# A hybrid decoder step: attention values two units behind their scores, the gate's projection partly between the dilated units, and the sample's values in three buffers

## What is computed

```python
u = rmsnorm(x) @ w_in                       # 1024 -> 4992 columns, 13 slabs of 384
# gated recurrence (hgrn), 6 heads: output o_a, gate g = silu(u[:, gate slab])
# differential attention, 6 heads, two maps, 512 keys, causal
a = softmax(q1 k1) - lam * softmax(q2 k2);  o_b = a @ v
# dilated sliding windows, 4 heads, dilations 1, 4, 16, merged by their denominators
o_c = sum_g w_g * (softmax(q_g k_g) @ v_g)
mix = concat(rmsnorm(o_a) * g, rmsnorm(o_b) * c, o_c)
h = x + mix @ w_out
h = h + experts(rmsnorm(h))                 # 16 experts, 2 of them for each token
y = final_norm(h + sigmoid(rmsnorm(h) @ pgw) * (p @ ppw))
```

## Time and profile before

| what | us |
|---|---|
| median of 3 runs (lowest, highest) | 1104.04 (1103.67, 1109.15) |
| time of the profiled execution | 1108.18 |
| its span | 1106.4 |
| TensorE busy / weight loads | 1039.1 (94%) / 542.3 |
| VectorE, ScalarE, GpSimd busy | 367.7, 249.1, 91.1 |
| DMA | 214.92 MB, mean 194 GB/s |

### The profile page before, as it was taken

The page is one execution under the profiler, slowest core; times in us unless marked ns, Lnnn a source line. Parts: engine busy times, 40 slices in busy tenths (PEclk is TensorE's granted clock), DMA queues, the critical chain, the costliest instruction groups (busy, mean ns, idle before and its releaser), DMA issues.

```text
span 1106.4 us, 11357 instructions
## 1 busy us (share of the span) xinstructions
PE 1039.1 (94%) x4147; PEld 542.3 (49%) x4147; DVE 367.7 (33%) x766; ACT 249.1 (23%) x577; POOL 91.1 (8%) x113
## 2 busy tenths in 40 slices
PE   6998999999998999888899969999999999998896
PEld 3444455544454765564644544444444444444342
DVE  5017436533225557255631341111011110100453
ACT  3043222211222322442421110001000100011454
POOL 1000000000005342010010010000000000001200
PEclk9998999988999999989999969999999999999999
DMA  6735303304346462346353285689998999886401
GB/s 200 285 133 162 131 3 133 133 3 164 133 139 230 153 212 61 113 154 198 122 199 123 77 318 194 241 305 343 350 345 305 343 348 341 286 330 250 134 20 57
DMA packets 97099, 214.92 MB, mean 194 GB/s; under 512 B 14481, under 2 KB 42996, under 8 KB 96668
## 3 DMA queue, kind: packets, MB, share of 16 engines
q1 hardware_dynamic: 86288, 185.78, 47.9%
q0 software_dynamic: 5616, 19.89, 5.0%
q10 hardware_dynamic: 5148, 8.63, 2.1%
HBM read 191.97 MB, written 41.14 MB: 211 GB/s over the span
## 4 chain that ended last, share of the span: by engine, by line
PE 81%; DVE 7%; DMA 3%; ACT 3%; SPq 2%; issue 2%; POOL 1%; ACTq 0%; DVEq 0%; POOLq 0%
PE ps L1967 15%; PE ps L2393 10%; PE ps L2423 10%; PE ps L2399 10%; PE ps L1972 7%; PE ps L2292 5%; PE ps L2488 5%; PE ps L2262 2%; PE ps L2003 2%; PE ps L1975 2%; PE ps L2049 1%; PE ps L2076 1%; PE ps L2188 1%; PE ps L1978 1%; SPq L636 1%
## 5 line engine op out<-in xcount | busy, mean ns | idle before, releaser
L1967 PE MATMUL ps<-xT,EXPERT 128*128 128x512 f32 x384 | 184.1, 623 | 1.5 <-DVE EXPERT L1298 1.5
L1972 PE MATMUL ps<-EXPERT,xT 128*128 128x384 f32 (+1 forms) x384 | 119.6, 454 | 0.0
L2393 PE MATMUL ps<-EXPERT,aF 128*128 128x512 f32 x256 | 114.7, 601 | 1.3 <-DVE aF L1856 1.3
L2423 PE MATMUL ps<-EXPERT,dF 128*128 128x512 f32 x256 | 112.6, 593 | 1.6 <-ACT dF L1171 1.6
L2399 PE MATMUL ps<-EXPERT,aF 128*128 128x512 f32 x256 | 112.5, 592 | 0.0
L1967 PEld LDWEIGHTS ps<-xT,EXPERT 128*128 128x128 f32 x384 | 71.3, 197 | 82.2 <-issue 79.0
L1972 PEld LDWEIGHTS ps<-EXPERT,xT 128*128 128x128 f32 x384 | 78.1, 237 | 25.6 <-issue 3.6
L2393 PEld LDWEIGHTS ps<-EXPERT,aF 128*128 128x128 f32 x256 | 49.4, 193 | 63.8 <-issue 62.1
L2423 PEld LDWEIGHTS ps<-EXPERT,dF 128*128 128x128 f32 x256 | 48.6, 190 | 62.6 <-issue 60.7
L2399 PEld LDWEIGHTS ps<-EXPERT,aF 128*128 128x128 f32 x256 | 47.4, 190 | 53.6 <-issue 53.6
L2488 PE MATMUL ps<-EXPERT 128*128 128x512 f32 x128 | 56.0, 594 | 2.7 <-DVE EXPERT L1913 2.7
(11 more groups left out here) (431 smaller groups left out, 1174.3 us busy)
## 6 DMA issues: line engine op xcount, KB each, us to landing
EXPERT<-in_moe_w_gate SPq DMA_DIRECT2D x16, 2048.0 KB, 15.1
EXPERT<-in_moe_w_up SPq DMA_DIRECT2D x16, 2048.0 KB, 20.0
EXPERT<-in_moe_w_down SPq DMA_DIRECT2D x16, 2048.0 KB, 10.0
EXPERT<-in_w_in SPq DMA_DIRECT2D x13, 1536.0 KB, 6.8
out_win_sample<-in_cache_win SPq DMA_DIRECT2D x16, 1022.0 KB
Yd<-wk ACTq DMA_DIRECT2D x16, 512.0 KB, 8.4
aF<-in_cache_k_diff SPq DMA_DIRECT2D x32, 192.0 KB, 2.5
aF<-in_cache_v_diff SPq DMA_DIRECT2D x32, 192.0 KB, 2.5
```

Of the source, the lines that this page charges most:

```text
L1967: last = t.matmul(ps[:, u % 2, :], W_[:, c, c0:c0 + w], xT[:, c, 0:SEQ], start=(c == 0), stop=(c == DC - 1))
L1972: last = t.matmul(ps[:, u % 2, 0:w], rows_, W_[:, c, c0:c0 + w], start=(c == 0), stop=(c == DC - 1))
L2393: last = t.matmul(ps[:, 2 + 2 * b, :], xgT[b][:, c, :], wg_[b][:, c, :], start=(c == 0), stop=(c == DC - 1))
L2423: last = t.matmul(ps[:, 6 + hf, :], hT[b][:, c, :], wd_[b][:, c, hf * 512:(hf + 1) * 512], start=(c == 0), stop=(c == FC - 1))
```

## The change

It sets the transposes two units behind the scores and the value products three, in both attention stages, with three probability buffers; takes the maximum of unit n before `weigh(n-1)`; splits `dec_new` in `dec_pre` and a short `dec_new`; moves `dec_soft` to the end of the differential stage (in banks 2 and 3 instead of 0 and 1, so that dilated unit 0 uses banks 4 and 5, and unit 1 waits for the sample's maxima); leaves the last fifteen parts of the gate's slab (ten of tokens, four of samples and the sum) for the first dilated units, two after each step; gives the sample's values a third buffer; gives key rows four stages; loads `w_out` as three chunks, two later (`w_more`) and three (`w_rest`); moves `gate_fn` behind `dec_v(1)`, `gate_mul` behind `dec_v(3)` and the readouts behind `dec_v` 5, 8, 11 and 14; and keeps the residue statistics in a small tile, so that each store of `res_d` is two transfers. The dilated units come out like this: projection up to unit 4; `krows` and `dec_wt` in units 4 and 5; `dec_v(0)` in unit 6; `gate_fn` in unit 7; readouts in units 10, 12, 14 and 15.

```diff
-D_SHARE = 1.7
+D_SHARE = 1.55
+C_SHARE = 2
-Q_LAG, Q_EVERY = 11, 5
+Q_LAG, Q_EVERY = 16, 4
-BUSY = 4
-RO_EVERY = 10
+BUSY = 3
...
-        if 1 <= n <= nd:
-            d.append(("d_t", n - 1))
-        if n >= 2:
-            d.append(("d_pv", n - 2))
+        if 2 <= n < nd + 2:
+            d.append(("d_t", n - 2))
+        if n >= 3:
+            d.append(("d_pv", n - 3))
...
+    side = [("krows", u) for u in range(KR_EARLY)] + [("dec_wt",)] + [("dec_v", u) for u in range(2 * NS)]
+    beside = {("dec_v", 1): ("gate_fn",), ("dec_v", 3): ("gate_mul",)}
+    beside.update({("dec_v", 5 + 3 * i): ("ro", i) for i in range(NT)})
...
+        if fresh == 2 and todo[0][0] > summed[10] + 1:
+            fresh = 1
+            steps.append(("dec_pre",))
+        if fresh == 1 and todo[0][0] > summed[12]:
+            fresh = 0
             steps.append(("dec_new",))
...
+        if st == ("d_pv", nd - 2):
+            steps.append(("dec_soft",))
...
+    def beside_units():
+        kind = side.pop(0)
+        steps.append(kind)
+        if kind[0] == "dec_v" and kind[1] % 2:
+            b = kind[1] // 2
+            if b + 3 < NS:
+                steps.append(("cached", b + 3, 1))
+            if b + 4 == NS:
+                steps.append(("w_rest",))
+            if b == 3 * (NS // 3) - 1:
+                steps.append(("w_more",))
+        if kind in beside:
+            steps.append(beside.pop(kind))
+        return kind[0]
+
+    free = 0
     for k, st in enumerate(c):
         steps.append(st)
+        if k == 1:
+            steps.append(("dec_norm",))
         if todo:
+            for _ in range(min(C_SHARE, len(todo))):
+                project_one()
+            if not todo:
+                steps += [("cached", 2, 1), ("outputs",)]
+                free = k + 1
+        elif side and k >= free:
+            free = k + C_PACE.get(beside_units(), 1)
...
             def cached(b, kv):
-                buf, ld = b % 2, kvload[b % 2]
+                buf = b % 3 if kv else b % 2
+                ld = vload[buf]
                 if kv == 0 and b >= 2:
                     sp.wait_ge(S_["kused"], b - 1)
                 elif kv == 1 and b < 2:
                     sp.wait_ge(S_["kused"], NS - 1 + b)
+                elif kv == 1 and b == 2:
+                    sp.wait_ge(S_["unit_pe"], NU)
                 elif kv == 1:
-                    sp.wait_ge(S_["pv_pe"], 2 * (b - 1))
+                    sp.wait_ge(S_["pv_pe"], 2 * (b - 2))
...
-                    pool.dma_start(res_d.rearrange("(s r) n -> r s n", r=4)[x], resid[:, x]).then_inc(S_["res_st"], 16)
+                    to = res_d.rearrange("(s r) n -> r s n", r=4)[x]
+                    pool.dma_start(to[:, 0:256], resid[:, x]).then_inc(S_["res_st"], 16)
+                    pool.dma_start(to[:, 256:CW], rst[:, x]).then_inc(S_["res_st"], 16)
...
             def d_s(n):
-                if n:
-                    weigh(n - 1)
                 K = (n // HB + 1) * P
...
                                 AX.X, ALU.max, negate=True).then_inc(S_["d_max"], 1)
+                if n:
+                    weigh(n - 1)
...
-                elif n >= 2:
+                elif n == 1:
+                    pe.wait_ge(S_["row_ok"], 1)
+                else:
                     pe.wait_ge(S_["c_exp"], n - 1)
...
-                for _ in range(BUSY):
+                for _ in range(BUSY if n >= 4 else 0):
                     t.matmul(ps[:, 6, 0:2 * P], identb[:], mband[:], start=True, stop=True)
...
             def krows(u):
                 i, groups = KU[u]
                 if u == 0:
-                    pe.wait_ge(S_["row_ok"], 1)
+                    pe.wait_ge(S_["unit_ok"], NU)
...
             def dec_soft():
                 pe.wait_ge(S_["kused"], NS)
                 pe.wait_ge(S_["dec_row"], 1)
-                pe.wait_ge(S_["unit_ok"], NU)
+                pe.wait_ge(S_["d_exp"], NT * HB - 1)
```

More of the change, by code:

```diff
@@ new lines, in schedule @@
+        if fresh == 1 and todo[0][0] > summed[12]:
+            fresh = 0
+            steps.append(("dec_new",))
+        if st == ("d_t", nd - 2):
+            steps += [("dec_q", b) for _, b in keys] + [("cached", b + 2 - NS, 1) for _, b in keys]
+            keys = []
+        if st == ("d_pv", nd - 2):
+            steps.append(("dec_soft",))
+    assert not fresh and todo
+    def beside_units():
[12 more added lines that the diff above has]
+        return kind[0]
@@ L252, in schedule @@
[L252 to L257, removed]
-    for kind in side:
-        steps.append(kind)
-        if kind[0] == "dec_v" and kind[1] % 2 and kind[1] // 2 + 2 < NS:
-            steps.append(("cached", kind[1] // 2 + 2, 1))
+            for _ in range(min(C_SHARE, len(todo))):
+                project_one()
@@ L262, in schedule @@
+            if not todo:
[3 more added lines that the diff above has]
+            free = k + C_PACE.get(beside_units(), 1)
+    while side:
+        beside_units()
     steps.append(("dec_out",))
-    steps += [("ro", i) for i in range(n_ro, NT)]
     late = [("krows", u) for u in range(KR_EARLY, n_kr)]
@@ L371, in hybrid_kernel @@
         stK = work2.rearrange("p (b c v) -> p b c v", b=NS, c=3)
-        part = [kdil[0].rearrange("p g n -> p (g n)")[:, 0:SLAB], work[:, 2 * SEQ:2 * SEQ + SLAB]]
+        part = [kdil[0].rearrange("p g n -> p (g n)")[:, 0:SLAB], spart[:]]
+        wrow = wk[:].rearrange("p a n -> p (a n)")
+        dP = [wrow[:, k * 2 * SEQ:(k + 1) * 2 * SEQ] for k in range(3)]
+        cP = [wk[:, 0, 0:SEQ], wk[:, 1, 0:SEQ], wk[:, 0, SEQ:2 * SEQ]]
         kpage = [aF_[:, k * PAGES * SLAB:(k + 1) * PAGES * SLAB].rearrange("p (j n) -> p j n", j=PAGES)
                  for k in range(2)]
+        kv3 = EXPERT[:, DC * SLAB:DC * SLAB + PAGES * SLAB]
+        kd3 = EXPERT[:, DC * SLAB + PAGES * SLAB:DC * SLAB + PAGES * SLAB + 512]
+        vpage = kpage + [kv3.rearrange("p (j n) -> p j n", j=PAGES)]
+        vdil = [[k[:, g] for g in range(NG)] for k in kdil] + [[kd3[:, 0:256], kd3[:, 256:512], spart[:, 0:256]]]
+        LAST3 = max(b for b in range(NS) if b % 3 == 2)
         NQ = SLAB + NG * 256
@@ L562, in hybrid_kernel @@
         KPER = 2 * PAGES // 2 + NG
+        V3_LOADS = 16 * KPER * len([b for b in range(NS) if b % 3 == 2])
         Q_STORES = 16 * 10
@@ L662, in outputs, with w_rest, w_more @@
                             out(rows_, cvT[:, g, i])
-            does = dict(slab=load_slab, copy=copy, state_in=state_in, state_out=state_out, q_out=q_out, cached=cached,
+            def w_rest():
+                wo = a["w_out"][0].rearrange("(c p) n -> p c n", p=P)
+                sp.wait_ge(S_["c_s_pe"], NCU // 2)
+                sp.wait_ge(S_["kr_pe"], KR_EARLY)
+                for c in range(WO_NOW, DC):
+                    sp.dma_start(wout_[c], wo[:, c]).then_inc(S_["woload_last"], 16)
+            def w_more():
+                sp.wait_ge(S_["pv_pe"], 2 * (LAST3 + 1))
+                wo = a["w_out"][0].rearrange("(c p) n -> p c n", p=P)
+                sp.dma_start(EXPERT[:, WO_FIRST * D:WO_NOW * D].rearrange("p (c n) -> p c n", c=WO_NOW - WO_FIRST),
+                             wo[:, WO_FIRST:WO_NOW]).then_inc(S_["woload"], 16)
+            does = dict(w_more=w_more, w_rest=w_rest, slab=load_slab, copy=copy, state_in=state_in, state_out=state_out, q_out=q_out, cached=cached,
                         outputs=outputs)
@@ L1684, in _ @@
             does = dict(act_fn=act_fn, log_f=log_f, gate_fn=gate_fn, lev_d=lev_d, lev_q=lev_q, lev_cp=lev_cp, io_a=io_a, io_b=io_b, h_state=h_state,
-                        d_s=d_s, d_t=d_t, c_s=c_s, c_pv=c_pv, dec_new=dec_new, dec_q=dec_q, dec_soft=dec_soft, dec_norm=dec_norm, gate_mul=gate_mul,
+                        d_s=d_s, d_t=d_t, c_s=c_s, c_pv=c_pv, dec_pre=dec_pre, dec_new=dec_new, dec_q=dec_q, dec_soft=dec_soft, dec_norm=dec_norm, gate_mul=gate_mul,
                         dec_wt=dec_wt, dec_v=dec_v, dst_v=dst_v, dst_new=dst_new, dst_o=dst_o, dec_sum=dec_sum, ro=ro)
```

166 lines of the change are left out of this document (75 added, 91 removed).

## The result

The changed kernel took 1111.25 us (median of 20 runs), the kernel before, on the same chip, 1105.79 (20 runs): ratio 1.005, 95% interval 1.0032 to 1.0068. It is slower by half a per cent, where I had forecast 1% faster: +5.5 us in place of -10.2. The profiled execution took 1110.56 us, its span is 1108.8.

A forecast was written before the change was run, and what follows sets the result against it. TensorE was taken as the bound, with 32 of 289 us in waits and low clock. Terms 171.2 + 22.2 + 27.5 + 42.7 + 5.5 + 9.8 = 278.9 against 289.1, -10.2 us, gave 1093.8 us; range 1080 to 1104.

The forecast's parts named there:

- the pace of the key buffers: Differential stage: an 18.3 us round for two samples just fits 2 times 9; priced at nothing, at most 1.5 us each.
- Rival C: Differential stage: `dec_q` becomes the pace, loads meet others, six samples 1.5 us late each, 9 us; 1103 us, chance 0.16.
- the moved gate parts: Differential stage: 17.4 us of gate slab leave it, not saved but done between dilated units 0 to 4; stage 171.2 us.
- units 0 to 3: First dilated units: 5.6 us of their own and 16.6 of projection, 22.2 us, with no wait.
- the third unit of distance: Differential stage: a late VectorE can catch up; 5.7 us of waits and 1.9 of clock go, 1.0 left for remnants.
- Units 4 to 9: Dilated stage: 24.1 us of work plus waits, together 27.9, taken as 27.5 us.
- The value buffers: Dilated stage: three buffers for the sample's values remove the 5.0 us of waits for values.
- The last stretch: Unit 10's scores to last value product: 30.3 us of work, 12.4 of waits, 5.5 of clock; VectorE's load 39.2.
- my sign: Last stretch: TensorE waits for merges 10 us or more in all, at units 10, 12, 14; VectorE over 0.85 busy.
- A: Last stretch: VectorE's pile does not hold TensorE back, 38.1 in place of 48.2 us; 1083.7 us, chance 0.24.
- The low clock: Last stretch: for 12 us of waits, the worst earlier rate, 0.13 x 42.7 = 5.5 us.
- Rival B: Last stretch: clock falls with the first wait and stays at 1.2 GHz, +18 us; 1111.6 us, chance 0.10.

The follow-up runs named there:

- e14: Changed kernel with GpSimd's two large products of each sample replaced by five plain fills of the same length: 1104.82 us, 0.999 of the kernel before.
- e8: Changed kernel, `dec_q` at 11 and 5, differential transposes one unit behind scores, value products two, weighing before maximum: 1108.53 us, 0.998 of the kernel before.
- e4: Changed kernel with `dec_q` at the old 11 and 5, and gate function, its scaling and readouts moved: 1092.64 us, 0.985 of the kernel before.
- e2: Kernel before with only the new cadence of `dec_q`, first after 16 steps, then every 4: 1114.19 us, 1.005 of the kernel before.
- e6: Changed kernel with `dec_q` first 11 steps after `q_out`, but still every 4 steps: 1110.01 us, 1.000 of the kernel before.
- e16: Changed kernel with `dec_q` at 11 and 5, but `dec_q(4)` alone three steps earlier: 1102.39 us, 0.992 of the kernel before.
- e1: Changed kernel with only `dec_q` back at the old cadence, first after 11 steps, then every 5: 1097.98 us, 0.990 of the kernel before.
- e17: Changed kernel in which GpSimd first frees VectorE, then multiplies as much on an unread tile, a repeat run: 1103.42 us, 0.995 of the kernel before.

## Why the prediction was wrong, step by step

**The step that failed** is the pace of the key buffers: "18.3 us for two samples, against 2 times 9. So the pace just holds, and I price it at nothing, with up to 1.5 us for each of six samples as the upper end." The round trip was right: 19.0 us from `dec_q(2)` to `dec_q(4)`. What it was held against was wrong in two ways. First, 18 us was twice an average of TensorE's work over four steps; VectorE has nothing to wait for inside a unit and reaches `dec_q` as soon as its unit's weighing is done, so the distance comes in whole units, two or three, and a pair two units apart has 10 to 13 us here, not 18 (10.1 and 10.7; in e14, with no weighing held up, 12.3 and 10.8). Second, a product of GpSimd holds up the weighing ahead of `dec_q`, so that a buffer is freed late while the next use comes on time. The two together made 9 us at each of two samples, not 1.5 at six, and 15 us of stage. Rival C had the place right, `dec_q` as the pace, but priced it at 9 us in all, and its reason, loads that meet others, is not what the changed kernel's rows show: its round trip at sample 4 was 15.6 us, as before. Its chance of 0.16 was too low for a balance that I had myself put at 18.3 against 18. My range reached 1104 and had to reach past 1111.

**What held.** The waits of the earlier trace rows went: at the old pace none is left, and the clock is 1.00. That stage sums to what I said for the moved gate parts (172.2 for 171.2), and units 0 to 3 ran without a wait at full clock (20.3 for 22.2). But the third unit of distance did more than I had priced (e8). Units 4 to 9 came to 27.4 for 27.5, in part by luck: 2.4 us of idle time for my 3.8, and a clock of 0.94 that I hadn't counted. ScalarE's block with the two table loads took 4.4 us again (491.01 to 495.41). The Trainium skill (ScalarE: Activation LUTs, What ACT_TABLE_LOAD costs) would, by an estimate from its figure, have put 2.7 us on top of that. The value buffers left 2.9 us of waits for values against 5.0 in the earlier trace rows, not none as I had said.

**What held only as a sum.** The last stretch is 48.0 for 48.2, but VectorE was busy 32.3 us where I had 39.2, 0.67 and not over 0.85; the waits for merges were 7.1 us at value products 10 and 14 where I had 9.8 at three places, and all idle time came to 11.0 for 12.4. With waits under 10 us neither my sign nor A's (under 5) was met. The low clock cost more than its 5.5 us: granted 0.83, over 48 us, is 8. The readouts' place was a real loss, shown by e4. The tail ran at 0.84 in place of 1.00, 1.9 us that I had not counted: the last merge's wait of 5.2 us lies just ahead of it.

**Rival B** did not come: 0.83 in the stretch, not under 0.7. Its 1111.6 us is the measured time by chance alone; the loss lies in the differential stage, where B had none. With the Trainium skill's rule that was weighed for it (TensorE: Matmul & The Clock Gate, HAM oscillation) the trace agrees in direction only: with four waits of 1.3 to 5.2 us and some short ones the stretch fell to 0.83.

**Left open:** why close pairs have 15.9 to 18.9 us in e2 and e6 and 10 to 13 in the changed kernel, e14 and e16; how TensorE's stops and its lower clock divide between the length and the slowing, of which only VectorE's waits are divided above; why the first stretch of the program, with the same steps, moves the start of the stage by 2 us and more.

## What to carry to other kernels

When two buffers feed a step that a second engine does in a fixed place of its program, compare the round trip with the shortest distance between two uses, in that engine's own program, not with an average of the bottleneck's work; one added condition in the scheduler (three units apart) does for a quick cadence what a slower cadence does. In e14 and e16 one delay of about a unit was hidden or nearly so, and a second before the engine had caught up was not: delays that seem free alone add up. And a part of a change that is priced at "just holds" deserves an experiment or a chance of one half.

## What the runs showed of the hardware

In these traces a VectorE operation with two inputs in SBUF, the on-chip memory, stands until GpSimd's product ends. In the rows of e8 above an 8 by 96 product that takes 0.24 us when GpSimd is idle (in e1, below) took 3.37, and ended at 402.34, 0.1 us behind GpSimd's; the next ended at 403.75, beside GpSimd's end at 403.5. In the same way the weighing's last operation on 128x384 took 3.73 us for 0.62 (368.51 above). Its first, a tensor times a column of scalars, was held too: 2.40 us for 0.42 in e17 at 365.82. Reductions were not held up (1.75 us each time), and beside fills, which read nothing, the weighing's last operation was as quick as ever (e14: mean 619 ns for 128x384; changed kernel: 1343), though its first took 1.25 us for 0.49 once (e14, 394.23):

```profile
393.30 0.24 DVE L1569 TENSOR_TENSOR EXPERT<-EXPERT,ident 8x96 f32<-8x96 f32 x1
```

The weighing's last operation between 320 and 440 us, by shape (busy us, mean ns, idle), in the changed kernel and in e14:

```profile
L1512 DVE SCALAR_TENSOR_TENSOR wk<-wk,small 128x384 f32<-128x384 f32 x6 | 8.1, 1343 | 0.2
```

```profile
L1512 DVE SCALAR_TENSOR_TENSOR wk<-wk,small 128x384 f32<-128x384 f32 x6 | 3.7, 619 | 0.2
```

The Trainium skill (SBUF — State Buffer, Who interferes with whom) states just this: a VectorE instruction with two SBUF inputs contends with a GpSimd instruction that reads SBUF, not with one that only writes it, and the second to come blocks until the first ends. The traces agree in each of these parts. I had not drawn on it in the prediction, though it bears on the weighing beside every product.
